# Moving a few tiles by 64 to 320 bytes within each SBUF partition, with no instruction changed

## The reference

```
# block 1
h = rmsnorm(x, norm_mix);  proj = h @ w_in            # 1024 x 9488
y_a = mamba2(...);  y_b = moba(...);  y_c = forgetting(...);  y_d = sliding_window(...)
x = x + sum_i(sigmoid(gate_i) * (y_i @ w_branch_i)) @ w_out
x = x + (silu(h2 @ w_gate) * (h2 @ w_up)) @ w_down    # h2 = rmsnorm(x), 2816 wide
x = rmsnorm(x, norm_final)
# block 2, twice: a mixer (HGRN2, then a gated linear recurrence), then a SwiGLU of 2816
x = x + mixer(rmsnorm(x)) ;  x = x + swiglu(rmsnorm(x))
return rmsnorm(x, norm_final_2)
```

## The kernel before, in words

| tile | before | after | moved by |
|---|---|---|---|
| `raw`, `whi`, `wlo`, `x_sb` | 0 | 0 | 0 |
| `hn` | 0 | 64 | 64 |
| `eh`, `el` | 0 | 0 | 128 |
| `hh`, `hl` | 32 | 32 | 128 |
| `wrow` | 32 | 0 | 224 |
| `ident`, `vec`, `st` | 32 | 64 | 288 |
| `diag` | 0 | 64 | 320 |
| `half` | 0 | 0 | -1920 |
| `gate`, `bh`, `bl`, `area`, `ring`, `gh`, `gl`, `qT`, `og`, `ch`, ... | as before | as before | 0 |

## Time and profile before

### The profile page before, as it was taken

One profiled execution on the slowest core, in us unless ns is written; L12 is line 12 of the kernel. 1 busy time (PEld: TensorE's weight loads), 2 busy tenths in 40 slices (PEclk: granted clock), 3 DMA queues, 4 the chain that ended last, 5 costly groups with the idle time before them and its releaser, 6 DMA issues.

```text
span 1134.9 us, 19300 instructions
## 1 busy us (share of the span) xinstructions
PE 1120.9 (99%) x8117; PEld 1042.9 (92%) x8117; DVE 660.1 (58%) x1039; ACT 574.5 (51%) x878; POOL 296.4 (26%) x193
## 2 busy tenths in 40 slices
PE   8999999999999999999999999999999999999997
PEld 7899989999989999889998889999889979999986
DVE  6755755677676454338898675443337797434324
ACT  6646555555445544436742544444435855544432
POOL 3022100000005445422421205444420003444440
PEclk9999999999999999999999999999999999999999
DMA  8689474544646666664553348665555255666550
GB/s 265 209 254 329 139 239 143 164 151 138 201 159 207 195 178 204 201 197 150 175 177 115 111 150 272 212 189 192 194 184 183 96 175 160 212 191 191 188 185 37
DMA packets 155152, 207.48 MB, mean 183 GB/s; under 512 B 9471, under 2 KB 128409, under 8 KB 155066
## 3 DMA queue, kind: packets, MB, share of 16 engines
q1 hardware_dynamic: 151274, 193.11, 54.5%
q0 software_dynamic: 3792, 13.15, 3.5%
HBM read 205.01 MB, written 4.24 MB: 184 GB/s over the span
## 4 chain that ended last, share of the span: by engine, by line
PE 89%; DVE 7%; ACT 3%; issue 1%; DMA 0%; POOL 0%; SPq 0%; DVEq 0%; ACTq 0%
PE bank L492 18%; PE bank L500 18%; PE bank L495 18%; PE bank L520 9%; PE bank L516 9%; PE bank L512 9%; PE bank L861 3%; DVE wlo L1359 2%; PE bank L787 1%; PE bank L797 1%; ACT whi L958 1%; DVE area L1507 1%; PE bank L562 1%; PE bank L809 1%; DVE uc L1507 0%
## 5 line engine op out<-in xcount | busy, mean ns | idle before, releaser
L1359 DVE TENSOR_TENSOR wlo<-raw,whi 128x1024 fp32r<-128x1024 f32 x275 | 336.0, 1250 | 233.0 <-ACT whi L958 232.1
L958 ACT ACTIVATE whi<-raw 128x1024 fp32r<-128x1024 f32 x362 | 360.3, 1044 | 111.7 <-PE bank L520 106.8
L1947 POOL TENSOR_TENSOR wlo<-raw,whi 128x1024 fp32r<-128x1024 f32 x87 | 222.7, 2560 | 250.9 <-ACT whi L958 250.8
L492 PE MATMUL bank<-hh,whi 128*128 128x256 f32 x1784 | 285.0, 281 | 0.0
L500 PE MATMUL bank<-hl,whi 128*128 128x256 f32 x1784 | 281.2, 279 | 0.0
L495 PE MATMUL bank<-hh,wlo 128*128 128x256 f32 x1784 | 281.2, 279 | 0.0
L492 PEld LDWEIGHTS bank<-hh,whi 128*128 128x128 f32 x1784 | 240.4, 188 | 3.3 <-issue 2.7
L495 PEld LDWEIGHTS bank<-hh,wlo 128*128 128x128 f32 x1784 | 239.9, 188 | 0.0
L500 PEld LDWEIGHTS bank<-hl,whi 128*128 128x128 f32 x1784 | 239.8, 188 | 0.0
L1954 POOL TENSOR_TENSOR st<-st,half 128x1 f32<-128x1 f32 x18 | 10.8, 608 | 334.9 <-DVE st L1376 302.6
L512 PE MATMUL bank<-whi,gh 128*128 128x512 f32 x264 | 81.5, 390 | 0.0
(11 more groups left out here) (313 smaller groups left out, 1227.8 us busy)
## 6 DMA issues: line engine op xcount, KB each, us to landing
raw<-in_ffn_w_in SPq DMA_DIRECT2D x88, 512.0 KB, 3.7
raw<-in_w_in SPq DMA_DIRECT2D x72, 512.0 KB, 4.9
raw<-in_ffn_w_out SPq DMA_DIRECT2D x44, 512.0 KB, 3.3
raw<-in_hgrn_w_in SPq DMA_DIRECT2D x32, 512.0 KB, 4.4
raw<-in_w_ffn_gate SPq DMA_DIRECT2D x22, 512.0 KB, 4.5
raw<-in_w_ffn_up SPq DMA_DIRECT2D x22, 512.0 KB, 4.5
raw<-in_w_ffn_down SPq DMA_DIRECT2D x22, 512.0 KB, 3.3
raw<-in_w_branch SPq DMA_DIRECT2D x16, 512.0 KB, 4.5
```

Source lines behind the costliest of these rows:

```text
L492: T.matmul(out, wh[:, i, c], xh[:, k, :], start=first and (i, k) == pairs[0], stop=False)
L958: A.activation(half_of(whi, j, h), half_of(raw, j, h), ACT.Copy).then_inc(s_hi[j % NS][h], 1)
L1359: V.tensor_tensor(half_of(wlo, j, h), half_of(raw, j, h), half_of(whi, j, h).bitcast(f32), ALU.subtract).then_inc(s_lo[j % NS][h], 1)
L1947: G.tensor_tensor(half_of(wlo, j, 1), half_of(raw, j, 1), half_of(whi, j, 1).bitcast(f32), ALU.subtract).then_inc(s_lo[j % NS][1], 1)
```

## The change

Five unused gap tiles are added or resized and `half` is moved ahead of `ident`. All tiles from `gate` on stay where they were. The instructions of all five engines, their order, shapes and waits are word for word the same in both kernels; only addresses differ, as in the table above. No row of the order moves, so none is shown here.

```diff
         x = sbuf(root, "x_sb", [128, 2, D])
+        sbuf(root, "gap_hn", [128, 16])
         hn = sbuf(root, "hn", [128, 2, D])
         shifted = ExitStack()
+        sbuf(shifted, "gap_eh", [128, 16])
         eh = sbuf(shifted, "eh", [128, 8, 256], f32r)
         el = sbuf(shifted, "el", [128, 8, 256], f32r)
         shifted.close()
-        sbuf(root, "gap_hh", [128, 8])
+        sbuf(root, "gap_hh", [128, 24])
         hh = sbuf(root, "hh", [128, 8, 256], f32r)
         hl = sbuf(root, "hl", [128, 8, 256], f32r)
+        sbuf(root, "gap_wrow", [128, 24])
         wrow = sbuf(root, "wrow", [128, 2, D])
+        half = sbuf(root, "half", [128, 16])
         ident = sbuf(root, "ident", [128, 128])
         vec = sbuf(root, "vec", [128, 128])
         st = sbuf(root, "st", [128, 24])
+        sbuf(root, "gap_diag", [128, 8])
         diag = sbuf(root, "diag", [128, 2, 128])
-        half = sbuf(root, "half", [128, 16])
-        sbuf(root, "gap_stage", [128, 80])
+        sbuf(root, "gap_stage", [128, 16])
```

## The result

The changed kernel takes 1141.62 us (median of 4 runs, 1141.56 to 1141.90) against 1136.13 (4 runs, 1136.07 to 1136.31): ratio 1.0047 [1.0035, 1.0059], slower by 5.5 us, or 0.5%. The forecast was no change, 1136.2 us, with a range up to 1139.5, so it was wrong: the change is clear of the noise and lies outside the range. The profiled execution took 1141.56 us, its span is 1140.3 us.

The account below looks back on a forecast made before the run. TensorE, busy 1120.9 of 1134.9 us, was taken as the bound: number of matmuls times their pace. All terms were taken as 0, so 1136.18 + 0 = 1136.2 us, with an 8-in-10 range of 1133.8 to 1139.5.

Parts of the forecast that it names:

- term 1: Big products with `hh`, `hl`, `eh`, `el`: moving by 128 leaves their pace unchanged; taken as 0, bounds -19 to +5 us.
- term 2: Transpositions against `ident`, some 180: taken as 0, with ends of -0.5 and +0.4 us.
- Rival D: Big products: address period longer than 128, -19 to +5 us; upper half plus unpriced 0.08, lower half plus Rival C 0.12.
- Rival A: Stream behind the factors' product (L570) comes out at the slower 117.7 ns: +3.0 us, 1139.4 us; in full 0.10.
- Rival B: Transpositions leave the stream at 116.7 ns more often: -1.0 us, 1135.2 us; inside the 0.70 for all terms small.
- Rival C: 256-column stream reaches 113 ns: -10.8 us behind L570, -19 us in all products; 0.12 with lower half of Rival D.
- Terms 2 to 5: Transpositions, factors' product, VectorE/ScalarE/GpSimd work and DMAs: each taken as 0, small ends together -0.7 and +0.8 us.

Follow-up runs that it names:

- the third experiment: Kernel before with only `hh` and `hl` moved by 128 bytes, small tiles behind carried along by 128: 1140.29 us, ratio 1.0035.
- the fourth: Kernel before with `eh` and `el` moved by 128 bytes, `hh` and `hl` and the small tiles behind by 256: 1137.40 us, ratio 1.0008.
- The sixth experiment: Kernel before with `hh` and `hl` 0 instead of 32 bytes behind the weights modulo 256, small tiles moved by 256: 1149.45 us, ratio 1.0117.
- the tenth: Kernel before with `hh` and `hl` 192 instead of 32 bytes behind the weights modulo 256, small tiles moved by 256: 1130.56 us, ratio 0.9952.
- the first experiment: Changed kernel with `hh`, `hl`, `eh`, `el` back at their old places modulo 256, small tiles' changes modulo 128 left: 1135.91 us, ratio 0.9997 to before.
- fifth experiment: Kernel before with every tile, weights included, moved by 128 bytes through a gap ahead of `raw`: 1136.07 us, ratio 0.9999.
- the second: Kernel before with `hh`, `hl`, `eh` and `el` moved by 128 bytes, small tiles behind carried along, `hn` staying: 1141.16 us, ratio 1.0043.

## Why the prediction was wrong

**The step that failed is term 1**, "The big products", taken as 0 and measured +5.6 us: +4.3 for `hh`/`hl` moving, +0.9 for `eh`/`el`, +0.4 for `bh`/`bl`. The condition it rested on, "if the pace depends on addresses modulo 128 or less", is false. Distance 160 gives 117.3 ns against 116.7 at 32 (the third experiment), 96 gives 120.0 against 118.3 at 224, and a move of 256 brings 116.7 back (the fourth). A period of 256 fits all that was tried.

**What was offered for it did not bear on it.** The equal 0.87 us of eight transpositions with `area` at 64 and `og` at 128 come from fp32 blocks with 128 columns moving, and the two places are 64 apart and not 128. After the change `ident` had moved by 288 bytes against them and they took 0.87 us again, so that row tells no address from another. The nearest rows were those of the big products: `hh` and `eh` in the 512-column form, which the prediction used only for an end of term 2 and to weigh a rule of the Trainium skill. The sixth experiment shows that the place makes their difference: `hh` at distance 0 takes 226.7 ns as well. And `bh` at 113.1 stood at a distance of its own.

The prediction drew from the Trainium skill (TensorE: Matmul & The Clock Gate, Part 2: two independent read ports, so that a weight load takes no read bandwidth from the running matmul) that the pace is the same at every place. That does not hold: the kernels above run from 1130.6 to 1151.8 us with the same instructions, and the measurement decides. Whether the ports are the reason no run shows.

**Rival D was right in mechanism**, with 0.08 for its slower half and whatever else was not priced. Its +5 us was worked out for `hh` and `hl` moving, which measured +4.3; `eh` and `bh` had no price and bring the sum to +5.6. That +5 held here was luck: it was taken from the slower gait seen before (117.7), and there are slower ones (118.5 here, 120.0 elsewhere), so that at distance 96 the same matmuls cost +15.7. Its mark was the right one: L512's counterpart with `eh` went from 227.3 to 232.3 ns. Nothing measured spoke for a period of 128, so the chance was too low; with no row on either side D deserved about an even chance.

**Rival A did not happen.** Behind L574, the factors' product in the changed kernel, the stream still comes out in the faster of its two gaits, now 117.3 instead of 116.7. From the timeline:

```profile
682.69 0.64 PE L504 MATMUL bank<-hl,whi 128*128 128x256 f32 x4
...
685.54 0.64 PE L504 MATMUL bank<-hl,whi 128*128 128x256 f32 x4
686.01 0.61 PE L574 MATMUL bank<-ident,diag 128*128 128x128 f32 x4
...
687.40 0.63 PE L504 MATMUL bank<-hl,whi 128*128 128x256 f32 x4
...
707.11 0.63 PE L504 MATMUL bank<-hl,whi 128*128 128x256 f32 x4
```

(2.85 / 24 = 118.8 ns ahead of it, where the earlier trace rows gave 117.8, and 19.71 / 168 = 117.3 behind it.) Both gaits have become slower, which A did not foresee. What A describes exists elsewhere: the stream behind L571 is in the slower gait in one mixer of the fourth experiment and in two feed-forward layers of the tenth. Its price was a little low too, since by the starts 984 matmuls (115 us, not 105) follow L570 in each feed-forward layer: some 371 us with the mixers, +3.2 us. **Rival B** happened in the first experiment, where it is worth 0.4 us. **Rival C** did not happen in the changed kernel, but its pace exists for `hh`: 113.3 ns over a whole feed-forward layer at distance 192, which the prediction held against it ("no stretch of `hh` shows 113").

**Terms 2 to 5** were right at 0: transpositions 0.87 us for 8, VectorE 684 and 692 ns, and all small tiles together -0.3 us (the first experiment), which is within the noise. What no term foresaw is that a stream's gait can change though neither of its tiles moved: `bh` in the first branch went from 113.1 to 117.8 ns. By the starts in their traces its first part stayed at 113.3 where `hh` has its old distance (the first, fourth and fifth experiment) and went to 117.8 in all others but the tenth, where `hh` has another one. So the gait of `bh` can change with the place of `hh`, which runs before it and which it does not read. In the second and third the second part stayed at 113.3 and the first part of the next branch went from 117.8 to 113.3, so that in sum nothing was lost; the changed kernel has both parts of the first branch at 117.8 without a gain elsewhere. What its small tiles add to that was not tried alone.

## What to carry to other kernels

Where TensorE is full of fp32r products with 256 columns, the distance between the stationary and the moving tile modulo 256 bytes is a tuning knob. Here 1.9% lies between the worst and the best place, and 0.5% between the kernel before and the best. It is cheap to scan: move one tile in steps of 16 or 32 bytes and read the pace from the starts of the matmuls. Never take an address change as free because it keeps some remainder, unless a row of the same form of matmul shows that remainder to be the one that counts. And a gain from a gait that short fp32 matmuls switch on and off has to be measured again after each change of the order.

## What was not expected of the hardware

- The pace of the 256-column stream took, with the same instructions in every kernel, the values 113.3, 116.7, 117.3, 117.8, 118.3, 118.7 and 120.0 ns in its feed-forward layers and mixers, by distance and gait. It is not monotone: whole kernels at distances 0, 16, 32, 48, 64, 96, 160, 192 and 224 take 1149.5, 1137.9, 1136.2, 1142.8, 1139.1, 1151.8, 1140.3, 1130.6 and 1142.8 us. Distance 128 was not tried for `hh`.
- With 512 columns moving the order is another: 226.7 ns at distance 0, where 256 columns are at 120.0, then 229 at 192, 232 to 233.5 at 16, 32, 48, 64, 128, 160 and 224, and 234.2 at 96.
- In the 256-column stream of the kernel before (380 to 400 us) the records of weight loads fill 20.00 of 20.00 us; beside 512 columns of `eh` (315 to 330 us) they fill 12.42 of 15.00. That load and matmul read SBUF at the same time and get in each other's way by their relative place would fit this, and the fifth experiment, but no run here shows the reads themselves: it stays a guess, as does what decides between two gaits at one distance.
